# PEER dots that read the tile's activations from PSUM instead of SBUF, in a one-core DeepNorm encoder layer

## The chip, the cores and the metric

The kernel runs on one core of a Trainium2 chip. The metric is the device time of one execution in microseconds (us), smaller is better. Several executions are timed, and their median is the figure that is compared.

## What is computed

One post-norm encoder layer over 1024 positions of width 1024 in float32. The mixer half is multi-head attention (8 heads) beside a Fourier branch, merged by gates and projected. The second half is a retrieval layer (PEER), and it is where most bytes move: each position picks 128 of 16384 experts (8 heads, the best 16 each), and with its input `xc` (called h1 here), its experts `ec` and gates `gc`

```
u = jnp.take(w_u, ec, axis=0)
h = jnp.einsum('cd,ced->ce', xc, u, preferred_element_type=jnp.float32)
a = (jax.nn.gelu(h, approximate=False) * gc).astype(x.dtype)
return jnp.einsum('ce,ced->cd', a, jnp.take(w_v, ec, axis=0))
```

So every position needs 128 rows of `w_u` and 128 rows of `w_v`, each 4 KB, at data-dependent places.

## The kernel before, in words

The 1024 positions are four groups of 256; a group is two tiles of 128 positions (one position per partition). A prologue (input norm, latents, keys and values, Fourier branch) is followed by a long software pipeline. It is written out by hand as steps m = 0 to 255 per group: in step m of group g, every engine first does its part of one retrieval slot of group g and then its part of the front work (attention to routing) of group g+1. The instruction order of each engine is the order of these steps; the engines are held together by semaphores alone. A group before the first, called -1, runs only the front of group 0 beside the last part of the Fourier transform. The last group runs with no front beside it.

**The retrieval slots.** Slot i of a group is one expert per partition; slots 0 to 127 belong to tile 0, slots 128 to 255 to tile 1. For a slot, GpSimd (POOL) issues an indirect DMA for 128 rows of `w_u` (`gather_u`, L310, 76 slots ahead of m) and another for 128 rows of `w_v` (`gather_v`, L319, 64 ahead), both into rings of six buffers. Issuing one reads the column of row numbers `ids_peer` and makes the descriptors. VectorE (DVE) multiplies the landed u row by h1 and sums (`dot`, L872, in step m for slot m+76); its end frees the buffer for the gather six slots on. After eight dots ScalarE (ACT) does a Gelu, DVE multiplies by the gate (`coefs`, L883). ACT scales the v row into `av` (`scale`, L1099, two buffers), which frees the v buffer, and TensorE (PE) adds `av` to the accumulator in PSUM by eight transposing matmuls (L600).

**The front.** Attention goes head by head (u = 0 to 15: two tiles, eight heads), one head every four steps, in steps 0 to 70. Head u's steps, with a = 4u, are:

| step | engine and line | work |
|---|---|---|
| a (first tile only) | PE L467, DVE L752 to L755, ACT L1025 | queries of the head and their rotary part |
| a+2 | PE L483, DVE L760 | scores into `fA` (two banks), their maximum |
| a+3 | ACT L1030 | exponential of `fA` into `probs` |
| a+5 | PE L491 (recorded at its helper, L341), DVE L768 | `probs` turned into `fB` (two banks), copied to `probsT` |
| a+7 | PE L499 | probabilities times values |

So the next head's scores (step a+6) come one step after this head's turn. Steps 72 to 119 are gates and branch projections (L523, L535), 120 to 134 the output projection (L546), 136 to 146 the norm that gives h1, 148 to 212 the retrieval queries (L567) and key scores (L575). Weights come in 512 KB chunks through a ring of four. `retrieve` (DVE only, with `topk`, L734 to L742, and L813 to L861) finds the experts: tile 0 in steps 157 to 219, tile 1 in steps 27 to 117 of the following round, so beside the next group's attention. When the first quarter of a tile's lists is ready it copies h1 into `h1_peer` in SBUF (L855).

**PSUM** has eight banks, all of them in use: `acc` two (the retrieval accumulator), `fA` two, `fB` two, `m0` and `m1` one each. `m0` has the queries and the turned attention output, `m1` the attention output; both are free between step 72 and step 148.

Of the kernel before, what the change touches and what calls it, by code (L numbers as in the profile page):

```python
# [20 lines left out]
D = 1024  # L21
S = 1024
H, NOPE, ROPE, VD = 8, 64, 32, 64
# [7 lines left out]
KD = D // P  # L31
# [36 lines left out]
def layer_program(nc, x, lnp, w_lat, w_z, w_kr, b_lat, b_zT, b_krT, gqkv, w_uk, w_uv, b_gate, wstream,  # L68
# [4 lines left out]
    with ctx:  # L73
# [99 lines left out]
            return ctx.enter_context(nc.psum_tensor(name, [P, n], fp32))  # L173

        acc = ps("acc", D)
        fA, fB = ps("fA", 1024), ps("fB", 1024)
        m0, m1 = ps("m0", 512), ps("m1", 512)
        banks = (fA[:, 0:512], fA[:, 512:1024], fB[:, 0:512], fB[:, 512:1024])

        cos_part, sin_part = acc[:, 0:512], acc[:, 512:1024]  # L180

# [155 lines left out]
        def _(pe):  # L337
# [108 lines left out]
            def front(g, m):  # L446

                for u in range(TILES * H):
                    a = A0 + A_PERIOD * u
                    qt, h = divmod(u, H)  # L450
                    if m == a and qt == 0:
                        c0 = WQ0 + 2 * (h // 4)
                        if h == 0:
                            pe.wait_ge(q_in, 32 * g + 32)
                        if h % 4 == 0:
                            chunk(g, c0)
                            chunk(g, c0 + 1)
                        if positive(g * H + h):
                            pe.wait_ge(q_nope, g * H + h)
                        if positive(g * H + h):  # L460
                            pe.wait_ge(q_rope, g * H + h)
                        if h == 0:
                            if positive(g * 2 * PH):
                                pe.wait_ge(s_sb, g * 2 * PH)
                        o = (h % 4) * P
                        for k in range(2):
                            last = mm(m0[:, 0:GROUP], wring[:, (c0 + k) % NW, o:o + P], cqT_g[:, k, :],  # L467
                                      start=k == 0, stop=k == 1)
                        last.then_inc(q_ps, 1)
                        if h % 4 == 3:  # L470
                            pe.drain().then_inc(w_free, 1)
                            pe.drain().then_inc(w_free, 1)
                    if m == a + 2:
                        if qt == 0:
                            pe.wait_ge(q_nope, g * H + h + 1)
                            pe.wait_ge(q_rope, g * H + h + 1)
                        if positive(g * TILES * H + u):
                            pe.wait_ge(probs_sb, g * TILES * H + u)
                        if u == 0:
                            if positive(g * TILES):  # L480
                                pe.wait_ge(h1T_sb, g * TILES)
                        for half in range(2):
                            last = mm(fA[:, half * 512:(half + 1) * 512], qT_g[0:QK, h, tok(qt)],  # L483
                                      KT[0:QK, h, half * 512:(half + 1) * 512], start=True, stop=True)
                        last.then_inc(scores_ps, 1)
                    if m == a + 5:
                        pe.wait_ge(probs_sb, g * TILES * H + u + 1)
                        if positive(g * TILES * H + u):
                            pe.wait_ge(probsT_sb, g * TILES * H + u)
                        for k in range(TT):  # L490
                            last = tr(fB[:, tok(k)], probs[:, tok(k)])  # L491
                        last.then_inc(probsT_ps, 1)
                    if m == a + 7:
                        pe.wait_ge(probsT_sb, g * TILES * H + u + 1)
                        if h == 0:
                            if positive(g * TILES + qt):
                                pe.wait_ge(o_done, g * TILES + qt)
                        for k in range(TT):
                            last = mm(m1[:, h * VD:(h + 1) * VD], probsT[:, tok(k)], V[:, k, h * VD:(h + 1) * VD],  # L499
                                      start=k == 0, stop=k == TT - 1)  # L500
                        last.then_inc(pv_ps, 1)
                    if h == H - 1 and m == a + 9:
                        pe.wait_ge(o_done, g * TILES + qt + 1)
                        if positive(g * TILES + qt):
                            pe.wait_ge(oT_sb, g * TILES + qt)
                        for c in range(4):
                            last = tr(m0[:, tok(c)], o_sb[:, tok(c)])
                        last.then_inc(oT_ps, 1)

                for dc in range(KD):  # L510
                    a = M0 + M_PERIOD * dc
                    gb, yb = banks[dc % 2], banks[2 + dc % 2]
                    for j in range(2):
                        if m == a + 2 * j:
                            if dc == 0 and j == 0:
# [23 lines left out]
                for k in range(KD):  # L539
                    if m == O0 + 2 * k:  # L540
                        if k == 0:
                            pe.wait_ge(m_done, (g + 1) * KD)
                        w = chunk(g, WO0 + k)
                        for t in range(TILES):
                            for half in range(2):
                                last = mm(banks[2 * t + half], mT[:, k, tok(t)], w[:, half * 512:(half + 1) * 512],  # L546
                                          start=k == 0, stop=k == KD - 1)
                        last.then_inc(w_free, 1)

                for t in range(TILES):  # L550
                    if m == L0 + 4 + 4 * t:
                        pe.wait_ge(h1_done, g * TILES + t + 1)
                        for k in range(KD):
                            last = tr((fA, fB)[t][:, tok(k)], h1_front[:, t, tok(k)])
                        last.then_inc(h1T_ps, 1)

                for qc in range(2 * PH):
# [73 lines left out]
        def _(dve):  # L631
# [112 lines left out]
            def front(g, m):  # L744
                for u in range(TILES * H):
# [18 lines left out]
                    if m == a + 5:  # L764
                        dve.wait_ge(probsT_ps, g * TILES * H + u + 1)
                        if positive(g * TILES * H + u):
                            dve.wait_ge(pv_ps, g * TILES * H + u)
                        v.tensor_copy(probsT, fB[:, :]).then_inc(probsT_sb, 1)  # L768
                    if h == H - 1 and m == a + 8:
                        dve.wait_ge(pv_ps, g * TILES * H + u + 1)  # L770
                        if positive(g * TILES + qt):
# [7 lines left out]
                for dc in range(KD):  # L779
                    if m == M0 + M_PERIOD * dc + 5:  # L780
                        dve.wait_ge(gates_sb, g * KD + dc + 1)
                        dve.wait_ge(w_free, used(g, WM0 + 3 * dc + 2))
                        v.tensor_tensor(prod[:, :, :].rearrange("p a b -> p (a b)"),  # L783
                                        sg[:, :, :].rearrange("p a b -> p (a b)"), banks[2 + dc % 2], ALU.mult)
                        dve.drain()
                        v.tensor_tensor(mT[:, dc, :], prod[:, 0, :], prod[:, 1, :], ALU.add).then_inc(m_done, 1)
                        dve.drain()
                for t in range(TILES):
                    if m == L0 + 4 * t:
                        if t == 0:  # L790
                            dve.wait_ge(w_free, used(g, WP0 - 1))
                            dve.wait_ge(hres_in, 16 * (g + 1))
                        v.tensor_tensor(h1_front[:, t, :], h1_front[:, t, :], (fA, fB)[t][:, :], ALU.add)
                        dve.drain()
                        stats(1, h1_front[:, t, :], var1)
                    if m == L0 + 4 * t + 2:
# [69 lines left out]
            def dot(g, i):  # L866
                g, i = slot_of(g, i)
                t = i // SLOTS
                dve.wait_ge(u_in[ring(g, i, NU)], landed(g, i, NU))
                row = u_rows[:, ring(g, i, NU), :]  # L870
                b = i // BATCH % 2
                v.tensor_tensor_reduce(out=row, in0=row, in1=h1_peer[:, t, :], scale=1.0, scalar=0.0, op0=ALU.mult,  # L872
                                       op1=ALU.add, accum_out=dots[:, b, i % BATCH:i % BATCH + 1]).then_inc(u_free, 1)

            def coefs(g, k):
# [68 lines left out]
        def _(act):  # L944
# [71 lines left out]
            def front(g, m):  # L1016
# [24 lines left out]
                for dc in range(KD):  # L1041
                    if m == M0 + M_PERIOD * dc + 3:
# [1 line left out]
                        if positive(g * KD + dc):  # L1044
                            act.wait_ge(m_done, g * KD + dc)
                        for j in range(2):
                            last = s.activation(sg[:, j, :], banks[dc % 2][:, j * GROUP:(j + 1) * GROUP], ACT.Sigmoid,
                                                bias=bg[:, j, dc:dc + 1])
                        last.then_inc(gates_sb, 1)
                if m == HAND1 + 2:  # L1050
# [4 lines left out]
                for t in range(TILES):  # L1055
# [2 lines left out]
                        s.activation(sd[:, 1, 1:2], sd[:, 1, 0:1], ACT.Sqrt).then_inc(std1, 1)  # L1058
                    if m == L0 + 4 * t + 6:
                        act.wait_ge(h1T_ps, g * TILES + t + 1)  # L1060
                        s.activation(hT_g[:, :, tok(t)], (fA, fB)[t][:, :].rearrange("p (k t) -> p k t", k=KD),  # L1061
                                     ACT.Copy).then_inc(h1T_sb, 1)
                for qc in range(2 * PH):
                    a = K0 + K_PERIOD * qc
# [182 lines left out]
```

## Time and profile before

| | |
|---|---|
| median of 3 runs | 3676.09 us (3662.14 to 3679.78) |
| profiled execution, its own time | 3666.81 us |
| its span, first to last instruction | 3665.0 us |
| PE matmul busy | 2779.8 us, 76% |
| POOL busy | 2356.0 us, 64% |
| DVE busy | 2220.9 us, 61% |
| ACT busy | 1612.2 us, 44% |
| bytes moved by DMA | 1240.83 MB, of them 1073.87 MB by POOL's gathers |

Busy time counts an instruction from its start to its end; waiting for a semaphore is not in it. The profile cuts the span into 40 slices: the DMA engines are busy from slice 7 on (about 550 us), when the first gathers go out, until the end, and move between 317 and 409 GB/s there. The first 550 us are the prologue and the front of group 0.

### The profile page before, as it was taken

What the parts mean: (1) busy time and instruction counts of PE and PEld (TensorE: products, weight loads), DVE (VectorE), ACT (ScalarE), POOL (GpSimd) and SP (SyncE); (2) the same over time, 40 slices, a digit from 0 to 9 for tenths busy, and PEclk for the clock granted to TensorE, in tenths of its full rate; (3) what the DMA queues carried; (4) which work ended last, traced back from release to release, by engine and by line L of the source; (5) the groups of instructions that cost most, each with busy time, mean ns of one, the idle gap of its engine ahead of it and who ended that gap; (6) DMA issues with size and microseconds to landing.
All of it is one profiled execution on the core that took longest, in us unless ns stands there. A gap on an engine that the chain in (4) does not pass through costs nothing.

```text
span 3665.0 us, 40824 instructions
## 1 busy us (share of the span) xinstructions
PE 2779.8 (76%) x14008; PEld 2205.7 (60%) x14008; DVE 2220.9 (61%) x5004; ACT 1612.2 (44%) x1842; POOL 2356.0 (64%) x2075
## 2 busy tenths in 40 slices
PE   6999986667788776677788776678787776666676
PEld 3456855556676565556675665567775665555555
DVE  5044148547865578457765686477765785466643
ACT  1121013445554555455554554455454454444444
POOL 3000007766677777766778787666777777777775
PEclk9999997578799898587899896687899985655556
DMA  4224539999999999999999999999999999999998
GB/s 170 92 92 144 172 125 341 384 344 327 330 399 409 409 409 386 376 340 317 360 409 409 409 393 376 374 338 328 373 409 409 409 382 373 408 364 357 359 396 344
DMA packets 350432, 1240.83 MB, mean 339 GB/s; under 512 B 38480, under 2 KB 46160, under 8 KB 349712
## 3 DMA queue, kind: packets, MB, share of 16 engines
q0 software_dynamic: 294912, 1073.87, 76.7%
q1 hardware_dynamic: 34096, 117.94, 8.8%
q10 hardware_dynamic: 21216, 46.40, 3.6%
q8 instruction: 111, 1.82, 0.2%
q14 instruction: 97, 0.79, 0.1%
HBM read 1222.33 MB, written 15.73 MB: 338 GB/s over the span
## 4 chain that ended last, share of the span: by engine, by line
POOL 29%; PE 24%; DMA 18%; issue 11%; DVE 8%; ACT 5%; DVEq 3%; SPq 0%; ACTq 0%; POOLq 0%
DMA rows<-in_peer_v,ids_peer 17%; POOL rows L310 15%; POOL rows L319 15%; PE acc L600 5%; ACT av L1099 4%; PE fA L483 3%; PE m L567 2%; PE fA L523 2%; PE m L371 2%; DVE small L760 2%; PE acc L589 1%; PE fB L341 1%; DVE rows L872 1%; PE m L467 1%; PE m L499 1%
## 5 line engine op out<-in xcount | busy, mean ns | idle before, releaser
L600 PE MATMUL acc<-ident,av 128*128 128x128 f32 x8192 | 1471.9, 340 | 762.1 <-ACT av L1099 747.5
L600 PEld LDWEIGHTS acc<-ident,av 128*128 128x128 f32 x8192 | 1212.0, 176 | 1036.0 <-ACT av L1099 965.1
L310 POOL DMA_INDIRECT rows<-in_peer_u,ids_peer x1024 | 1151.3, 1124 | 828.2 <-DVE ids_peer L852 348.9
L872 DVE CUSTOM_DVE_ANT_0 rows<-rows,hh 128x1024 f32<-128x1024 f32 x1024 | 1241.9, 1222 | 698.1 <-DMA rows<-in_peer_u,ids_peer 687.2
L1099 ACT ACTIVATE av<-rows,coef 128x1024 f32<-128x1024 f32 x1024 | 1164.2, 1145 | 1107.8 <-DMA rows<-in_peer_v,ids_peer 1001.6
L319 POOL DMA_INDIRECT rows<-in_peer_v,ids_peer x1024 | 1156.7, 1130 | 318.9 <-issue 278.1
L567 PE MATMUL m<-hT_g,wring 128*128 128x256 f32 x1024 | 254.3, 406 | 1.1 <-ACT hT_g L1061 1.1
L523 PE MATMUL fA<-hT_g,wring 128*128 128x256 f32 x1024 | 233.7, 383 | 0.0
L567 PEld LDWEIGHTS m<-hT_g,wring 128*128 128x128 f32 x1024 | 206.9, 208 | 31.2 <-ACT hT_g L1061 1.5
L523 PEld LDWEIGHTS fA<-hT_g,wring 128*128 128x128 f32 x1024 | 193.3, 193 | 24.9
L1030 ACT ACTIVATE S<-fA,small 128x1024 f32<-128x1024 f32 x64 | 71.3, 1114 | 266.1 <-DVE small L762 266.1
L499 PEld LDWEIGHTS m<-V,S 128*128 128x128 f32 x1024 | 128.9, 203 | 18.1 <-DVE S L768 10.9
L768 DVE COPY S<-fB 128x1024 f32<-128x1024 f32 x64 | 78.2, 1222 | 100.2 <-PE fB L341 98.6
L499 PE MATMUL m<-V,S 128*128 128x64 f32 x1024 | 130.4, 284 | 9.3 <-DVE S L768 9.3
L483 PE MATMUL fA<-KT,hT_g 96*128 96x512 f32 x256 | 122.8, 602 | 0.0
L535 PE MATMUL fB<-yo,wring 128*128 128x256 f32 x512 | 115.8, 379 | 0.0
L760 DVE TENSOR_REDUCE small<-fA 128x1 f32<-128x1024 f32 x64 | 78.3, 1223 | 53.0 <-PE fA L483 52.9
L535 PEld LDWEIGHTS fB<-yo,wring 128*128 128x128 f32 x512 | 95.4, 190 | 12.0
L1090 ACT ACT_TABLE_LOAD x76 | 97.5, 1283 | 1.4
L783 DVE TENSOR_TENSOR prod<-sg,fB 128x512 f32<-128x512 f32 x32 | 21.8, 682 | 121.5 <-PE fB L535 121.5
L1069 ACT ACTIVATE qcT<-m 128x256 f32<-128x256 f32 x64 | 24.5, 383 | 152.6 <-PE m L567 152.6
L341 PE MATMUL fB<-ident,S 128*128 128x128 f32 x512 | 88.1, 330 | 1.0 <-issue 0.8
(153 smaller groups left out, 2183.2 us busy)
## 6 DMA issues: line engine op xcount, KB each, us to landing
wring<-in_wstream SPq DMA_DIRECT2D x192, 512.0 KB
ln<-in_dft_seq ACTq DMA_DIRECT2D x32, 512.0 KB, 3.5
rows<-in_peer_u,ids_peer POOLq DMA_INDIRECT x1024, 7.1
rows<-in_peer_v,ids_peer POOLq DMA_INDIRECT x1024, 7.1
hT_g<-in_x SPq DMA_DIRECT2D x8, 512.0 KB, 3.6
hres_spill<-KT ACTq DMA_DIRECT2D x8, 512.0 KB, 2.7
hT_spill<-rows ACTq DMA_DIRECT2D x1, 4096.0 KB, 11.1
wring<-in_wstream SPq DMA_DIRECT2D x16, 256.0 KB
```

The source lines that it names most:

```text
L310: pool.indirect_dma_start(u_rows[:, ring(g, i, NU), :], None, peer_u, bass.IndirectOffsetOnAxis(ap=ids_peer[:, t, s:s + 1], axis=0)).then_ ...
L319: pool.indirect_dma_start(v_rows[:, ring(g, i, NV), :], None, peer_v, bass.IndirectOffsetOnAxis(ap=ids_peer[:, t, s:s + 1], axis=0)).then_ ...
L341: return nc.tensor.transpose(out_, in_, ident[:, :])
L483: last = mm(fA[:, half * 512:(half + 1) * 512], qT_g[0:QK, h, tok(qt)], KT[0:QK, h, half * 512:(half + 1) * 512], start=True, stop=True)
L499: last = mm(m1[:, h * VD:(h + 1) * VD], probsT[:, tok(k)], V[:, k, h * VD:(h + 1) * VD], start=k == 0, stop=k == TT - 1)
L523: last = mm(gb[:, j * GROUP:(j + 1) * GROUP], w[:, tok(k)], hT_g[:, k, :], start=k == 0, stop=k == KD - 1)
L535: last = mm(yb[:, j * GROUP:(j + 1) * GROUP], w[:, tok(4 * j + k)], src[:, k, :], start=k == 0, stop=k == 3)
L567: last = mm(m0[:, (qc % 2) * GROUP:(qc % 2 + 1) * GROUP], w[:, tok(k)], hT_g[:, k, :], start=k == 0, stop=k == KD - 1)
L600: last = mm(acc[:, tok(k)], av[:, i % NAV, tok(k)], ident[:, :], is_transpose=True, start=i % SLOTS == 0 and k % 4 == 0, stop=i % SLOTS == ...
L760: v.reduce_max(nmax[:, u % 2:u % 2 + 1], fA[:, :], AX)
L872: v.tensor_tensor_reduce(out=row, in0=row, in1=h1_peer[:, t, :], scale=1.0, scalar=0.0, op0=ALU.mult, op1=ALU.add, accum_out=dots[:, b, i ...
L1099: s.activation(av[:, i % NAV, :], v_rows[:, ring(g, i, NV), :], ACT.Copy, scale=coef[:, b, i % BATCH:i % BATCH + 1]).then_inc(scaled, 1)
```

## The change

The two banks of `fB` become `h1_ps`. Before the first dot of each tile DVE copies that tile's h1 from SBUF to `h1_ps`, and all 128 dots of the tile take it from there; the u row, in and out, stays in SBUF. What used `fB` has to move: the gates' partner banks, the output projection of tile 1 and its turned h1 go to `m0` and `m1`, which become one tensor `mB`. The turned probabilities go to `fA`, the banks of the scores, in the fronts of groups 1 to 3 (in the front of group 0, which ends its attention before the first dot, they stay where they were). For that PE gets a new wait: before the scores of head u it waits until head u-1's turned probabilities have been copied out of `fA` (`probsT_sb`).

```
-        fA, fB = ps("fA", 1024), ps("fB", 1024)
-        m0, m1 = ps("m0", 512), ps("m1", 512)
-        banks = (fA[:, 0:512], fA[:, 512:1024], fB[:, 0:512], fB[:, 512:1024])
+        fA, h1_ps, mB = ps("fA", 1024), ps("h1_ps", D), ps("mB", 1024)
+        m0, m1 = mB[:, 0:512], mB[:, 512:1024]
+        banks = (fA[:, 0:512], fA[:, 512:1024], h1_ps[:, 0:512], h1_ps[:, 512:1024])
+        fbanks = (fA[:, 0:512], fA[:, 512:1024], m0, m1)
+        def turned(g):
+            return h1_ps if isinstance(g, int) and g == 0 else fA
...
+                        if u > 0 and turned(g) is fA:
+                            pe.wait_ge(probsT_sb, g * TILES * H + u)
                         for half in range(2):
                             last = mm(fA[:, half * 512:(half + 1) * 512], qT_g[0:QK, h, tok(qt)],
...
-                            last = tr(fB[:, tok(k)], probs[:, tok(k)])
+                            last = tr(turned(g)[:, tok(k)], probs[:, tok(k)])
...
-                    gb, yb = banks[dc % 2], banks[2 + dc % 2]
+                    gb, yb = fbanks[dc % 2], fbanks[2 + dc % 2]
...
-                                last = mm(banks[2 * t + half], mT[:, k, tok(t)], w[:, half * 512:(half + 1) * 512],
+                                last = mm(fbanks[2 * t + half], mT[:, k, tok(t)], w[:, half * 512:(half + 1) * 512],
...
-                            last = tr((fA, fB)[t][:, tok(k)], h1_front[:, t, tok(k)])
+                            last = tr((fA, mB)[t][:, tok(k)], h1_front[:, t, tok(k)])
...
-                        v.tensor_copy(probsT, fB[:, :]).then_inc(probsT_sb, 1)
+                        v.tensor_copy(probsT, turned(g)[:, :]).then_inc(probsT_sb, 1)
...
                 dve.wait_ge(u_in[ring(g, i, NU)], landed(g, i, NU))
+                if i % SLOTS == 0:
+                    dve.drain()
+                    v.tensor_copy(h1_ps[:, :], h1_peer[:, t, :])
+                    dve.drain()
...
-                v.tensor_tensor_reduce(out=row, in0=row, in1=h1_peer[:, t, :], scale=1.0, scalar=0.0, op0=ALU.mult,
+                v.tensor_tensor_reduce(out=row, in0=row, in1=h1_ps[:, :], scale=1.0, scalar=0.0, op0=ALU.mult,
```

The gate and norm lines of DVE and ACT change their bank in the same way.

## Rows read from the trace of the kernel before

**Rows 1.** The page, costliest groups: line, engine, operation | busy us, mean ns | idle before
```profile
L310 POOL DMA_INDIRECT rows<-in_peer_u,ids_peer x1024 | 1151.3, 1124 | 828.2 <-DVE ids_peer L852 348.9
L872 DVE CUSTOM_DVE_ANT_0 rows<-rows,hh 128x1024 f32<-128x1024 f32 x1024 | 1241.9, 1222 | 698.1 <-DMA rows<-in_peer_u,ids_peer 687.2
...
L319 POOL DMA_INDIRECT rows<-in_peer_v,ids_peer x1024 | 1156.7, 1130 | 318.9 <-issue 278.1
...
L768 DVE COPY S<-fB 128x1024 f32<-128x1024 f32 x64 | 78.2, 1222 | 100.2 <-PE fB L341 98.6
```
**Rows 2.** Stretches: length; busy us (x) of PE, PEld, DVE, ACT, POOL; PEclk; DMA share, GB/s
```profile
548.00:650.00 102.00, 67.73 (x340) 56.96 (x339) 83.45 (x237) 38.20 (x50) 72.84 (x61) 0.77 0.94 349
650.00:757.00 107.00, 66.75 (x313) 53.77 (x313) 55.19 (x104) 48.03 (x47) 82.61 (x81) 0.63 1.00 388
...
1552.00:1802.00 250.00, 186.59 (x1086) 157.72 (x1086) 177.40 (x371) 131.34 (x149) 165.22 (x148) 0.80 0.94 334
1802.00:2037.00 235.00, 192.23 (x1064) 155.45 (x1063) 147.78 (x330) 119.57 (x125) 184.94 (x153) 0.96 1.02 405
2037.00:2164.00 127.00, 95.85 (x571) 82.85 (x570) 91.26 (x246) 63.83 (x78) 99.82 (x85) 0.93 1.02 401
2164.00:2256.00 92.00, 63.52 (x360) 53.84 (x359) 73.94 (x192) 48.21 (x56) 73.11 (x62) 0.82 0.99 379
2256.00:2344.00 88.00, 61.55 (x266) 49.32 (x266) 41.34 (x71) 38.26 (x37) 67.55 (x68) 0.56 1.02 400
...
757.00:1552.00 795.00, 608.28 (x3338) 507.08 (x3338) 531.13 (x1207) 401.12 (x444) 570.88 (x511) 0.83 0.98 376
1552.00:2344.00 792.00, 599.73 (x3338) 499.18 (x3338) 531.71 (x1207) 401.21 (x444) 590.64 (x514) 0.85 0.99 378
2344.00:3137.00 793.00, 604.33 (x3336) 504.45 (x3334) 531.32 (x1206) 400.44 (x444) 592.57 (x512) 0.84 0.98 376
...
3220.00:3480.00 260.00, 168.00 (x719) 134.94 (x717) 176.78 (x440) 115.16 (x114) 202.51 (x177) 0.54 0.97 358
3480.00:3554.00 74.00, 52.13 (x216) 41.64 (x216) 33.77 (x59) 32.24 (x31) 56.83 (x56) 0.52 1.00 392
3554.00:3634.00 80.00, 59.13 (x249) 47.28 (x250) 38.56 (x67) 36.16 (x36) 60.99 (x63) 0.54 1.03 409
```
**Rows 3.** The chain of waits, share by line, 3220 to 3480 us (last group)
```profile
by line: POOL rows L319 31.2%; POOL rows L310 26.9%; issue 17.2%; DMA rows<-in_peer_v,ids_peer 12.9%; ACT av L1099 2.2%; PE acc L600 0.8%; PE acc L607 0.8%; DVEq L850 0.6%; DVE onehot L840 0.5%; DVE ybuf L648 0.5%; DVE ybuf L888 0.5%; DVE y
```
**Rows 4.** The chain of waits, share by line, 1667 to 1776 us (attention of group 2)
```profile
by line: PE acc L600 17.9%; issue 10.3%; DVE rows L872 8.4%; PE fA L483 8.0%; DVE small L760 7.7%; PE fB L341 7.0%; ACT av L1099 4.8%; ACT L1090 2.3%; DVE S L768 2.2%; DVEq L811 2.1%; DVEq L735 2.1%; DVEq L737 2.0%; DVEq L739 1.9%; DVE si L
```
**Rows 5.** POOL's two lines over the whole run: ns min/median/max
```profile
L310 POOL DMA_INDIRECT rows<-in_peer_u,ids_peer x1024: 933/940/2130, 540.2 to 3627.4; - x171
...
L319 POOL DMA_INDIRECT rows<-in_peer_v,ids_peer x1024: 932/939/2202, 568.5 to 3645.4; - x171
```
**Rows 6.** Timeline at 1722.8 us: start us, us, engine, line (a gather issued beside a dot)
```profile
1722.86 1.22 DVE L872 CUSTOM_DVE_ANT_0 rows<-rows,hh 128x1024 f32<-128x1024 f32 x1
1722.90 1.98 POOL L310 DMA_INDIRECT rows<-in_peer_u,ids_peer  x1 [0.30 <-issue]
```
**Rows 7.** Timeline at 1226.4 us (a gather issued beside an SBUF plus PSUM sum)
```profile
1226.48 1.21 DVE L793 TENSOR_TENSOR hh<-hh,fB 128x1024 f32<-128x1024 f32 x1
1226.54 0.94 POOL L310 DMA_INDIRECT rows<-in_peer_u,ids_peer  x1 [0.30 <-issue]
```
**Rows 8.** Timeline at 2387 us, one head of attention: PE and DVE
```profile
2386.81 1.04 PE L341 MATMUL fB<-ident,S 128*128 128x128 f32 x8
...
2387.69 1.04 PE L600 MATMUL acc<-ident,av 128*128 128x128 f32 x8
2387.89 1.23 DVE L768 COPY S<-fB 128x1024 f32<-128x1024 f32 x1 [0.75 <-PE fB L341]
2388.45 0.30 PEld L483 LDWEIGHTS fA<-KT,hT_g 96*128 96x128 f32 x2
2388.56 1.88 PE L483 MATMUL fA<-KT,hT_g 96*128 96x512 f32 x4
...
2390.48 1.22 DVE L760 TENSOR_REDUCE small<-fA 128x1 f32<-128x1024 f32 x1 [0.23 <-PE fA L483]
```
**Rows 9.** Timeline at 2450 us, a head whose copy comes late behind retrieval
```profile
2450.58 0.30 PEld L483 LDWEIGHTS fA<-KT,hT_g 96*128 96x128 f32 x2
...
2454.38 1.22 DVE L768 COPY S<-fB 128x1024 f32<-128x1024 f32 x1
2455.66 2.65 PEld L499 LDWEIGHTS m<-V,S 128*128 128x128 f32 x13 [2.45 <-DVE S L768]
...
2456.66 1.22 DVE L760 TENSOR_REDUCE small<-fA 128x1 f32<-128x1024 f32 x1
```
**Rows 10.** DVE groups by shape: busy us, mean ns | idle before
```profile
L644 DVE SCALAR_TENSOR_TENSOR hh<-hh,small,ln 128x1024 f32<-128x1024 f32 x8 | 10.2, 1280 | 0.0
L888 DVE SCALAR_TENSOR_TENSOR ybuf<-hh,acc 128x1024 f32<-128x1024 f32 x8 | 9.7, 1218 | 20.9 <-PE acc L607 20.9
L855 DVE COPY hh<-hh 128x1024 f32<-128x1024 f32 x8 | 5.6, 696 | 0.0
```
**Rows 11.** Waits, 3220 to 3480 us: total us, times, longest
```profile
DVE rows L872 <- DMA rows<-in_peer_u,ids_peer: 67.8, 45, 2.5
```

More of the change, by code:

```diff
@@ L783, in front @@
                         v.tensor_tensor(prod[:, :, :].rearrange("p a b -> p (a b)"),
-                                        sg[:, :, :].rearrange("p a b -> p (a b)"), banks[2 + dc % 2], ALU.mult)
+                                        sg[:, :, :].rearrange("p a b -> p (a b)"), fbanks[2 + dc % 2], ALU.mult)
                         dve.drain()
@@ L792, in front @@
                             dve.wait_ge(hres_in, 16 * (g + 1))
-                        v.tensor_tensor(h1_front[:, t, :], h1_front[:, t, :], (fA, fB)[t][:, :], ALU.add)
+                        v.tensor_tensor(h1_front[:, t, :], h1_front[:, t, :], (fA, mB)[t][:, :], ALU.add)
                         dve.drain()
@@ L1046, in front @@
                         for j in range(2):
-                            last = s.activation(sg[:, j, :], banks[dc % 2][:, j * GROUP:(j + 1) * GROUP], ACT.Sigmoid,
+                            last = s.activation(sg[:, j, :], fbanks[dc % 2][:, j * GROUP:(j + 1) * GROUP], ACT.Sigmoid,
                                                 bias=bg[:, j, dc:dc + 1])
@@ L1060, in front @@
                         act.wait_ge(h1T_ps, g * TILES + t + 1)
-                        s.activation(hT_g[:, :, tok(t)], (fA, fB)[t][:, :].rearrange("p (k t) -> p k t", k=KD),
+                        s.activation(hT_g[:, :, tok(t)], (fA, mB)[t][:, :].rearrange("p (k t) -> p k t", k=KD),
                                      ACT.Copy).then_inc(h1T_sb, 1)
```

## The prediction

> **What bounds the kernel now.** I read the costliest groups first. POOL issues 1024 gathers for u and 1024 for v, at means of 1124 and 1130 ns; a dot on DVE takes 1222 ns [rows 1]. But half of all issues take 940 ns or less, and the longest over 2100 [rows 5]. The mean is pulled up by a part of the issues that are nearly a dot longer. The timeline shows which: an issue that starts 0.04 us after a dot takes 1.98 us [rows 6]. It ends 0.80 us after that dot does, as if it had got almost nothing done beside it. Next to a sum of the same size that has one input in SBUF and the other in PSUM, the issue takes 0.94 us [rows 7]. So what POOL waits for is DVE's second SBUF input. Over the run this is 1024 x (1124 - 940) + 1024 x (1130 - 939) ns = 384 us of POOL time.
>
> POOL is busy in 64% of the span, so next I asked where it is on the path. The table by stretches gives DMA's rate [rows 2]; 409 GB/s is the highest anywhere, and the reader should see that it is reached in quite different stages, so I take it as the ceiling. One steady group is 1552 to 2344 us; the two others (757 to 1552, 2344 to 3137) have its length within 3 us and its rate within 2 GB/s. Its attention (1552 to 1802) runs at 334 GB/s, the gates and projections at 405, the routing stretches at 401, 379 and 400. In the last group, with retrieval of tile 1 alone beside the slots (3220 to 3480), the rate is 358. There the chain of waits is POOL: 58% in its two lines and 17% in the issue time between them [rows 3]. In attention it is another chain: PE, DVE and ACT in turn, no POOL line among its leading entries [rows 4]. That is the ring scores, maximum, exponential, scaling, accumulating, turning, scores; a gather that comes earlier doesn't shorten it.
>
> **The change part by part.**
>
> *The dots free POOL (gain).* If issues fall to 940 ns beside every dot, POOL could do a slot in 2 x (0.94 + 0.30) = 2.48 us, the 0.30 being the issue gap [rows 6]. A slot's two gathers are 1.049 MB, 2.56 us at 409 GB/s, so DMA becomes the bound wherever POOL was. The most a stretch can give is its length x (1 - rate/409), for the same bytes. After attention in a steady group: 235 us at 405 gives 2.3, 127 at 401 gives 2.5, 92 at 379 gives 6.7, 88 at 400 gives 1.9; 13.4 together, 40 for three groups. Last group: 260 at 358 gives 32.4, 74 at 392 gives 3.1; 36. First slots: 107 at 388 gives 5.5, and 102 at 349 gives 15, of which I take a third, for DVE is 82% busy there [rows 2]. Upper end 96 us. A check from the other side: in 3220 to 3480 POOL's 177 issues took 202.5 us and would take 166, 36 us less, of which the ceiling lets 32 through. I take 85% of 40 and 36, since DVE's retrieval bursts leave gaps: 34 + 31 + 5 + 5 = 75 us. Lower end: half, 38.
>
> *Attention gets a link (loss).* Before, scores of head u+1 went into `fA` while head u's turned probabilities lay in `fB`. Now they wait for DVE's copy. In an ordinary head [rows 8] the turn ends at 2387.85; PE does a slot's accumulation meanwhile and loads weights for the scores at 2388.45. The copy ends at 2389.12, and PE starts about 0.05 after a copy's end, from 2455.60 to 2455.66 in [rows 9]. So the scores start at 2389.17, 0.72 later. DVE had nothing to do but wait for them, so the maximum comes 0.72 later, and with it the whole ring. Queued behind the waiting scores on PE are the next slot's accumulation and the value product, which waited for the same copy anyway. Where retrieval makes the copy late [rows 9], the scores wait 5.1 us (2450.58 to 2455.66), but DVE reaches the maximum late too: new scores end at 2457.5 against a maximum that began at 2456.66, 0.9 late. Other heads lie between 0.1 and 1.0; I take 0.65. Per group 15 heads have a predecessor, in three groups 45: 29 us. The front of group 0 keeps its old banks and costs nothing. Lower end: a third of it (10), should other slack in the ring take it up. Upper end: some four heads a group pass on 3 us each: 3 x (11 x 0.65 + 4 x 3) = 57.
>
> *The copies.* Eight, SBUF to PSUM, 128x1024. The trace has none; PSUM to SBUF takes 1222 ns [rows 1], SBUF to SBUF 696 [rows 10]. PSUM on one side makes the first the nearer; with two drains 1.4 us. The four for tile 0 (step 180) and the last for tile 1 lie where DVE waits for u rows (67.8 us in 260 in the last group [rows 11]) and cost nothing; without that cover each is 1.4 us. The three for tile 1 at step 52 fall into attention: about 1 us each, 3 us (0 to 4).
>
> *The dots themselves.* With a PSUM input a comparable two-input operation takes 1218 ns, with SBUF alone 1280 [rows 10]. The dot is at 1222 already; I leave it, between -60 and +60 ns. In attention 8.4% of the chain is dots [rows 4], so 5% on them is 3 us either way over 750 us; elsewhere they are covered. (The Trainium skill, VectorE: DVE Perf Modes, section on the TRN2 errata, gives VectorE a larger fixed cost from PSUM than from SBUF, 120 against 58 cycles at 0.96 GHz. By that estimate a dot is 65 ns longer and the sum 3 us worse; the rows on the sum with a PSUM input show no such excess.)
>
> *Moved banks.* Gates, output projection and the turned h1 use `m0` and `m1` when attention is over; their existing waits already cover it. Same instructions, same order: 0.
>
> **Sum.** -75 + 29 + 3 = -43 us on the profiled execution's own 3666.8 us: 3624. The median shown is 9 us higher; within that spread I give 3625.
>
> **The rivals.**
>
> *The late copies pass on in full.* Speaks for it: in attention everything hangs together, and retrieval is also on the chain. Against: the maximum was late as well [rows 9]. 3667 - 75 + 57 + 3 = 3652, no change.
>
> *The freed time stays off the path.* Only the lower gain comes, because gathers already fill DMA whenever they can. For it: DMA is called 97% busy even at 358 GB/s [rows 2]. Against: the chain there is POOL's. 3667 - 38 + 29 + 3 = 3661, no change.
>
> *Slower: the hold isn't lifted.* POOL would be held by the dot as such (its own kind of operation, u row in and out in SBUF), not by its second SBUF input. Then nothing is gained, and attention's link remains: 3667 + 32 = 3699. Rows 7 speak against it, but with a plain sum, not a dot. It decides if issues beside dots stay above 1100 ns in the mean. This is also how the change could fail to do what it says. (The Trainium skill, SBUF — State Buffer, section on who interferes with whom, says that a two-input VectorE operation holds up only GpSimd's reads, and infers that making descriptors needs only the write side and so isn't stalled by it. By that the change gains nothing, 3699 too. The 1.98 us issue beside a dot contradicts it, unless the reading of row numbers is what is held.)
>
> *Better: the link is hidden* in attention, or costs 10: 3667 - 90 + 10 = 3587.
>
> **How the numbers follow.** Forecast 0.60; late copies in full 0.13; gain off the path 0.10; hold not lifted 0.10; hidden link 0.07. Within 0.5% (18 us, about what this measurement tells from no change) lie the two middle rivals, less a part of each: 0.19. Slower: the third rival and the bad end of the second, 0.13. Faster: 0.68. Range: upper end of the gain with a small loss, 3590; above it takes in the late copies and the unhelped path, 3668. Left out are the hold not lifted and half of the best case.
>
> **What would show it.** Right: both POOL lines at about 940 to 960 ns in the mean; 3220 to 3480 shortened by some 28 us, at 400 GB/s or more; the attention stretch of each steady group longer by 9 to 12 us, with PE waiting for the copy in front of L483's line. Wrong: issue times as before; attention longer by 19 us or more; the rate still under 380 with fast issues, which would mean a loop between DVE and the six buffers bounds instead. Dots above 1290 ns would put retrieval on the path.

## The result and the profile after

The changed kernel takes 3636.6 us in the median (3625.2 to 3637.2, four runs) against 3677.9 for the kernel before in the same comparison (3662.1 to 3681.0); the ratio is 0.9885, 95% interval 0.9852 to 0.9917. That is 41 us less, and the interval of the ratio allows 31 to 54; 43 were forecast. The time itself was forecast at 3625 and is 12 us above it, nearly all because the prediction started from a profiled execution of 3666.8 us, which is 11 below the kernel's median here. The two profiled executions have spans of 3665.0 and 3634.6 us, only 30 apart, since the one of after lies at its kernel's median. Sums over stretches below are of those two.

The gather lines and the dot on the page after (line engine op, shapes and count | busy us, mean ns | idle before). They answer to [rows 1]; the code has moved, so L310 is L316, L319 is L325, L872 is L884:

```profile
L884 DVE CUSTOM_DVE_ANT_0 rows<-rows,h_ps 128x1024 f32<-128x1024 f32 x1024 | 1234.4, 1216 | 620.0 <-DMA rows<-in_peer_u,ids_peer 608.2
L316 POOL DMA_INDIRECT rows<-in_peer_u,ids_peer x1024 | 984.7, 962 | 1103.8 <-DVE dots L884 568.0
L325 POOL DMA_INDIRECT rows<-in_peer_v,ids_peer x1024 | 964.9, 942 | 371.1 <-issue 244.3
```

An issue takes 962 and 942 ns in the mean where it took 1124 and 1130. POOL got back 358 of the 384 us that the prediction counted, and what it got back became waiting for dots: 568 us, where it had been 203. The gathers go out earlier and stay under way longer, 11.9 us from issue to landing in the median for `w_u` rows, where it was 7.1. The dot is 6 ns shorter with its PSUM input.

The stretches of after (length; busy us of PE, PEld, DVE, ACT, POOL with counts; PEclk; DMA share, GB/s), cut at the same dots as those of before:

```profile
550.00:745.00 195.00, 126.58 (x646) 105.04 (x645) 137.39 (x339) 85.81 (x96) 136.57 (x144) 0.74 1.00 391
...
1542.00:1807.00 265.00, 191.62 (x1078) 155.01 (x1079) 178.88 (x372) 130.11 (x148) 136.09 (x143) 0.81 0.87 309
1807.00:2041.00 234.00, 191.50 (x1069) 154.91 (x1067) 146.46 (x329) 119.85 (x126) 145.42 (x153) 0.97 1.02 407
2041.00:2341.00 300.00, 216.85 (x1192) 182.78 (x1192) 206.79 (x508) 150.33 (x172) 206.70 (x218) 0.82 1.03 408
...
3216.00:3452.00 236.00, 154.76 (x715) 125.17 (x716) 176.74 (x443) 115.03 (x115) 168.06 (x177) 0.63 1.00 394
3452.00:3603.00 151.00, 112.28 (x471) 89.66 (x469) 72.62 (x125) 68.10 (x66) 107.72 (x115) 0.53 1.03 409
```

Against [rows 2], by the times of the same dots: the first slots gave 14 us (209 to 195, with 391 GB/s in place of 369), the stretches after attention 9, 8 and 12 us in the three groups, 28 before rounding (routing now at 406 to 409 GB/s), the last group 27 (of it 23 or 24 between 3216 and 3452). That is 69 us gained. The three attention stretches went the other way, from 253, 250 and 251 us to 265, 265 and 262: 36 lost by the dots' times, 38 by these whole numbers. The chain of waits of 3216 to 3452, which answers to [rows 3]:

```profile
by line: DMA rows<-in_peer_u,ids_peer 19.4%; POOL rows L316 11.9%; POOL rows L325 11.6%; issue 11.5%; DVE rows L884 8.9%; DMA rows<-in_peer_v,ids_peer 8.0%; DVEq L858 2.0%; DVEq L819 2.0%; DVEq L745 1.9%; DVEq L747 1.8%; DVE onehot L848 1.8
```

POOL's two lines fell from 58% to 24% of it; transfers and dots took over, and the rate of 394 is 15 under the highest.

One head of attention after, near the place of [rows 8] (timeline):

```profile
2398.08 1.04 PE L608 MATMUL acc<-ident,av 128*128 128x128 f32 x8
2398.28 1.23 DVE L776 COPY S<-fA 128x1024 f32<-128x1024 f32 x1 [0.68 <-PE fA L347]
...
2399.63 0.30 PEld L491 LDWEIGHTS fA<-KT,hT_g 96*128 96x128 f32 x2 [0.74 <-issue]
2399.66 1.95 PE L491 MATMUL fA<-KT,hT_g 96*128 96x512 f32 x4 [0.54 <-DVE S L776]
...
2401.65 1.22 DVE L768 TENSOR_REDUCE small<-fA 128x1 f32<-128x1024 f32 x1 [1.00 <-PE fA L491]
```

The copy ends at 2399.51 and the scores' weights are loaded at 2399.63. From the copy's start to that load it was 0.56 us in [rows 8]; here it is 1.35, so 0.79 more. DVE then waits 1.00 us for the scores, where it had waited 0.23.

A head whose copy comes late looks different. This is the head of [rows 9] in the changed kernel (timeline):

```profile
2456.74 1.20 DVE L776 COPY S<-fA 128x1024 f32<-128x1024 f32 x1
...
2458.09 3.75 PE L491 MATMUL fA<-KT,hT_g 96*128 96x512 f32 x4 [5.07 <-DVE S L776]
...
2461.88 1.23 DVE L768 TENSOR_REDUCE small<-fA 128x1 f32<-128x1024 f32 x1 [2.80 <-PE fA L491]
```

PE has waited 5.07 us for the copy, and then the scores take 3.75 us, where they took 1.88 before. The stretch of just these scores shows the TensorE clock that was granted, 0.50 of full speed, which is the 1.2 GHz level. The first line is of the changed kernel, the second of the same head's scores in the kernel before, at 1.00 (2.4 GHz):

```profile
2458.09:2461.84 3.75, 3.75 (x5) 1.58 (x6) 0.99 (x2) 0.00 (x0) 1.87 (x2) 0.50 0.71 234
```
```profile
2450.69:2452.57 1.88, 1.88 (x8) 0.87 (x7) 1.57 (x7) 0.97 (x1) 1.14 (x1) 1.00 0.95 373
```

So the next maximum begins 3.94 us after this copy's end; in [rows 9] it was 1.06. Taking the same times for all 45 heads that have a predecessor in their group (groups 1 to 3):

| mean, end of the copy to start of the next maximum | before | after |
|---|---|---|
| 33 heads, copy right behind the turn | 1.46 us | 2.17 us |
| 12 heads, four a group, copy late behind retrieval | 1.29 us | 3.87 us |

The 33 cost 0.71 each, the 12 cost 2.58 each: 23 + 31 = 54 us more at this link. Only 36 to 38 of it reached the length of attention; where the rest was made up isn't shown. In all of the 12, and in no head of the kernel before, the scores take over 3 us: PE has waited 3.0 to 5.4 us for the copy, and the clock is at 0.50 when they start (9 heads) or falls to it during them (3). The mean granted clock of the stretch did not fall (0.82, 0.81 and 0.84, before 0.77, 0.80 and 0.78); but slow moments now lie on the ring. In the chain of waits of 1660 to 1790 us the scores' line has 18.9%, where [rows 4] shows 8.0%.

### The profile page after: what moved, and what is told of

Same layout as the page of the kernel before. It is cut to its first block, busy times and chain, and to the rows that moved or that the text cites. A ratio compares the mean times of both kernels' runs of the same rounds, so it can differ in the third digit from the quotient of the medians.

```text
span 3634.6 us, 40893 instructions
## 1 busy us (share of the span) xinstructions
PE 2734.6 (75%) x14008; PEld 2148.4 (59%) x14008; DVE 2223.7 (61%) x5012; ACT 1610.4 (44%) x1842; POOL 1997.5 (55%) x2075
## 4 chain that ended last, share of the span: by engine, by line
PE 27%; DMA 26%; DVE 14%; POOL 12%; issue 9%; DVEq 6%; ACT 5%; SPq 0%; ACTq 0%; POOLq 0%
DMA rows<-in_peer_v,ids_peer 19%; POOL rows L316 6%; POOL rows L325 6%; DMA rows<-in_peer_u,ids_peer 6%; PE acc L608 5%; ACT av L1111 4%; PE fA L491 4%; PE fA L531 3%; DVE rows L884 3%; PE mB L575 2%; PE mB L543 2%; PE mB L377 2%; PE acc L597 2%; DVE small L768 1%; DVE S L776 1%
## 5 line engine op out<-in xcount | busy, mean ns | idle before, releaser
L608 PE MATMUL acc<-ident,av 128*128 128x128 f32 x8192 | 1408.9, 329 | 713.0 <-ACT av L1111 697.4
L884 DVE CUSTOM_DVE_ANT_0 rows<-rows,h_ps 128x1024 f32<-128x1024 f32 x1024 | 1234.4, 1216 | 620.0 <-DMA rows<-in_peer_u,ids_peer 608.2
L316 POOL DMA_INDIRECT rows<-in_peer_u,ids_peer x1024 | 984.7, 962 | 1103.8 <-DVE dots L884 568.0
L325 POOL DMA_INDIRECT rows<-in_peer_v,ids_peer x1024 | 964.9, 942 | 371.1 <-issue 244.3
L575 PE MATMUL mB<-hT_g,wring 128*128 128x256 f32 x1024 | 259.1, 411 | 1.1 <-ACT hT_g L1073 1.1
L575 PEld LDWEIGHTS mB<-hT_g,wring 128*128 128x128 f32 x1024 | 210.2, 211 | 32.8 <-ACT hT_g L1073 1.5
L507 PEld LDWEIGHTS mB<-V,S 128*128 128x128 f32 x1024 | 132.0, 207 | 10.1 <-issue 7.2
L507 PE MATMUL mB<-V,S 128*128 128x64 f32 x1024 | 132.0, 286 | 2.7 <-DVE S L776 2.7
L543 PE MATMUL mB<-yo,wring 128*128 128x256 f32 x512 | 115.8, 379 | 0.0
L543 PEld LDWEIGHTS mB<-yo,wring 128*128 128x128 f32 x512 | 95.4, 190 | 12.0
## 6 DMA issues: line engine op xcount, KB each, us to landing
rows<-in_peer_u,ids_peer POOLq DMA_INDIRECT x1024, 11.9
```

Of the source, the lines that this page charges most:

```text
L316: pool.indirect_dma_start(u_rows[:, ring(g, i, NU), :], None, peer_u, bass.IndirectOffsetOnAxis(ap=ids_peer[:, t, s:s + 1], axis=0)).then_ ...
L325: pool.indirect_dma_start(v_rows[:, ring(g, i, NV), :], None, peer_v, bass.IndirectOffsetOnAxis(ap=ids_peer[:, t, s:s + 1], axis=0)).then_ ...
L543: last = mm(yb[:, j * GROUP:(j + 1) * GROUP], w[:, tok(4 * j + k)], src[:, k, :], start=k == 0, stop=k == 3)
L575: last = mm(m0[:, (qc % 2) * GROUP:(qc % 2 + 1) * GROUP], w[:, tok(k)], hT_g[:, k, :], start=k == 0, stop=k == KD - 1)
L608: last = mm(acc[:, tok(k)], av[:, i % NAV, tok(k)], ident[:, :], is_transpose=True, start=i % SLOTS == 0 and k % 4 == 0, stop=i % SLOTS == ...
L884: v.tensor_tensor_reduce(out=row, in0=row, in1=h1_ps[:, :], scale=1.0, scalar=0.0, op0=ALU.mult, op1=ALU.add, accum_out=dots[:, b, i % BAT ...
```

## The experiments

**Dots from SBUF again (e1_sbuf_dots).** Banks, wait and copies stay as changed.

```
-  v.tensor_tensor_reduce(out=row, in0=row, in1=h1_ps[:, :], ...
+  v.tensor_tensor_reduce(out=row, in0=row, in1=h1_peer[:, t, :], ...
```

> The changed kernel with its banks, its new wait and its eight copies, but the dots read h1 from SBUF again. Theory (the dots' second SBUF input holds POOL's issues, and that is the whole gain; the wait in attention is the whole loss): both gather lines back at 1120 to 1135 ns in the mean, attention of each steady group still 261 to 265 us, the routing stretches and the last group as in the kernel before, the time about 3678 + 36 + 2 = 3716 us, ratio 1.008 to 1.012. Rival (the gain is from the moved banks, not from the operand): gather lines may be slow again but the time stays near 3637, ratio 0.99.

Measured: 3705.3 us against 3676.1 for the kernel before, ratio 1.0082 (1.0057 to 1.0107). The issues are slow again, 1110 and 1141 ns. Attention is nearly as long as in the changed kernel (784 us in the three stretches, there 792), and the last group is as in the kernel before; POOL's two lines are 64% of its chain again:

```profile
751.00:1014.00 263.00, 184.58 (x1077) 148.66 (x1078) 179.47 (x372) 130.01 (x148) 159.16 (x146) 0.84 0.88 316
1550.00:1812.00 262.00, 187.26 (x1073) 152.23 (x1073) 178.86 (x372) 129.60 (x148) 157.98 (x146) 0.82 0.89 317
2362.00:2621.00 259.00, 185.44 (x1073) 150.20 (x1072) 178.69 (x372) 129.64 (x148) 159.39 (x148) 0.83 0.89 321
3250.00:3509.00 259.00, 166.13 (x718) 133.48 (x719) 178.07 (x443) 115.28 (x115) 202.71 (x177) 0.55 0.97 359
```

It splits the change into its two parts: everything but the operand costs 29 us (the interval allows 21 to 39), and the operand alone gives 3705.3 - 3636.6 = 69. The two kernels were timed in different comparisons; by their ratios to the kernel before it is 72, give or take 15. The rival that the moved banks bring the gain is out. The loss is 9 us less than the 38 expected, inside the interval.

**The copy in two halves (e2_split_copy).** In the changed kernel, PE signals after four and after eight turns, DVE copies 512 columns at a time, and each half of the scores waits for its own half.

```
                         for k in range(TT):
                             last = tr(turned(g)[:, tok(k)], probs[:, tok(k)])
+                            if k % 4 == 3:
+                                last.then_inc(probsT_ps, 1)
...
-                            pe.wait_ge(probsT_sb, g * TILES * H + u)
+                            pe.wait_ge(probsT_sb, 2 * (g * TILES * H + u) - 1)
                         for half in range(2):
+                            if half == 1 and u > 0 and turned(g) is fA:
+                                pe.wait_ge(probsT_sb, 2 * (g * TILES * H + u))
...
-                        v.tensor_copy(probsT, turned(g)[:, :]).then_inc(probsT_sb, 1)
+                        for half in range(2):
+                            cols = slice(half * 512, (half + 1) * 512)
+                            dve.wait_ge(probsT_ps, 2 * (g * TILES * H + u) + half + 1)
...
+                            v.tensor_copy(probsT[:, cols], turned(g)[:, cols]).then_inc(probsT_sb, 1)
```

The other waits on these two semaphores count in twos as well.

> The changed kernel with each turned head copied out in two halves, signalled apart: the first half of the scores waits only for the first half's copy, and that copy starts after four of the eight turns. Theory (the scores' wait for the copy is what attention loses): the first half is free about 0.7 us earlier than the whole was, so most of the 0.7 to 0.8 us a head goes; attention 252 to 256 us a group instead of 261 to 265, the time 3637 - 25 = about 3612 us, ratio 0.980 to 0.985. Rival (attention lost its time through retrieval's late copies, or through gathers competing): attention stays at 260 or more and the extra 0.16 us of DVE a head makes the time 3637 to 3645, ratio 0.989 to 0.991.

Measured: 3597.8 us, ratio to the kernel before 0.9785 (0.9759 to 0.9811), whose interval lies wholly below that of the changed kernel. It beats both kernels: 78 us under the one before, 39 under the changed one. The attention stretches:

```profile
750.00:1002.00 252.00, 186.28 (x1080) 154.27 (x1078) 180.45 (x390) 130.61 (x148) 136.62 (x142) 0.81 0.90 329
1535.00:1790.00 255.00, 188.53 (x1074) 155.17 (x1074) 179.95 (x388) 129.73 (x148) 135.97 (x142) 0.80 0.89 320
2325.00:2576.00 251.00, 179.72 (x1079) 147.31 (x1078) 179.74 (x388) 130.26 (x148) 136.16 (x142) 0.84 0.90 324
```

They are 758 us together, where the changed kernel has 792 and the kernel before 754. One head there (timeline):

```profile
793.76 1.51 PE L347 MATMUL fA<-ident,S 128*128 128x128 f32 x8
794.86 1.29 DVE L781 COPY S<-fA 128x512 f32<-128x512 f32 x2 [1.61 <-PE fA L347]
795.88 0.30 PEld L493 LDWEIGHTS fA<-KT,hT_g 96*128 96x128 f32 x2
```

DVE starts copying at 794.86, before the eight turns are through at 795.27, and PE loads the scores' weights at 795.88, before both halves are out at 796.15. The scores are no longer behind the whole copy, and in the 33 ordinary heads PE no longer waits before them at all. In the 12 late ones it still waits, 2.8 to 5.3 us. The time gained is more than the 25 us expected. The profiled pair is 29 us apart, with 34 gained in attention; the difference to 39 is within what executions differ by. Heads whose scores take over 3 us are 7 here and 12 in the changed kernel, a part of the gain that the expectation didn't have; its size isn't separated.

**The copy a step later (e3_later_copy).** DVE copies the turned head at step a+6, behind the next dot.

```
-                    if m == a + 5:
+                    if m == a + 6:
                         dve.wait_ge(probsT_ps, g * TILES * H + u + 1)
```

> The changed kernel with DVE's copy of a turned head moved one step on, behind the next slot's dot. It doubles the suspected wait: the scores are later by a dot, 1.2 us, in each of 45 heads. Theory: attention longer by 45 x 1.2 / 3 = 18 us a group (279 to 283), the time 3637 + 54 = about 3690 us, ratio 1.000 to 1.006. Rival (the ring has slack and attention's loss is something else): under 5 us a group, the time under 3655, ratio under 0.995.

Measured: 3654.2 us, ratio 0.9932 (0.9907 to 0.9957), so 17.5 us above the changed kernel and neither theory's number. The three attention stretches are 270, 268 and 269 us, 15 more than in the changed kernel. Idle time of DVE ahead of the copy (us, times), changed kernel first, then this one:

```profile
  PE fA L347: 60.1, 33
...
  PE fA L491: 65.9, 43
```
```profile
  PE fA L347: 25.7, 17
...
  PE fA L491: 84.2, 44
```

The second line of each is PE waiting for the copy before the scores. In the changed kernel DVE often stood waiting for PE's turns; with the copy moved the dot sits in that gap and fills 34 us of it. 45 heads times 1.22 us is 55, less 34 is 21, near the 15 to 17.5 measured; PE's wait grew by 18. So the ring passes the delay on, but my count overlooked that a wait can be filled; delay counts only beyond the slack of the link it is put into.

**The product to PSUM (e4_product_to_psum).** Both inputs in SBUF, as before the change, only the write leaves SBUF. It has a drain before each dot and no copies of h1.

```
-                if i % SLOTS == 0:
-                    dve.drain()
-                    v.tensor_copy(h1_ps[:, :], h1_peer[:, t, :])
-                    dve.drain()
...
-                v.tensor_tensor_reduce(out=row, in0=row, in1=h1_ps[:, :], ...
+                dve.drain()
+                v.tensor_tensor_reduce(out=h1_ps[:, :], in0=row, in1=h1_peer[:, t, :], ...
```

> The dots take both inputs from SBUF and write the product to PSUM (with a drain in front of each dot, since all write the same place, and without the eight copies of h1). It tells the read side from the write side. Theory (the second SBUF input is what holds POOL): gather lines 1120 to 1140 ns in the mean, an issue beside a dot near 1.9 us, the time 3715 to 3740 us. Rival (the write of the product to SBUF, or its combination with two reads, holds POOL): gather lines 940 to 970 ns, the time 3640 to 3660 us.

Measured: 3696.2 us, ratio 1.0054 (1.0030 to 1.0078), and issues of 1116 and 1100 ns. The page's lines, then two moments of its timeline:

```profile
L316 POOL DMA_INDIRECT rows<-in_peer_u,ids_peer x1024 | 1143.1, 1116 | 891.2 <-DVE ids_peer L860 348.2
L881 DVE CUSTOM_DVE_ANT_0 h_ps<-rows,hh 128x1024 f32<-128x1024 f32 x1024 | 1264.3, 1235 | 662.7 <-DMA rows<-in_peer_u,ids_peer 577.0
L325 POOL DMA_INDIRECT rows<-in_peer_v,ids_peer x1024 | 1126.3, 1100 | 314.4 <-issue 235.2
```
```profile
769.41 1.23 DVE L881 CUSTOM_DVE_ANT_0 h_ps<-rows,hh 128x1024 f32<-128x1024 f32 x1
769.55 1.90 POOL L316 DMA_INDIRECT rows<-in_peer_u,ids_peer  x1 [4.94 <-DVE dots L881]
...
800.58 1.26 DVE L881 CUSTOM_DVE_ANT_0 h_ps<-rows,hh 128x1024 f32<-128x1024 f32 x1
800.58 0.94 POOL L325 DMA_INDIRECT rows<-in_peer_v,ids_peer  x1 [0.30 <-issue]
```

A dot that writes nothing big to SBUF holds an issue just as long: 1.90 us beside it. The changed kernel's dot has one read and the write in SBUF and doesn't hold it, so it is the two reads. The time is 19 us or more below what was expected, and 9 below e1_sbuf_dots; this kernel has no copies of h1 and its issues are a little shorter, and I did not take that difference apart.

**Splitting alone (e5_split_alone).** The kernel before, with only the halved copy and its signals, as in e2_split_copy (turned heads stay in `fB`, the scores don't wait).

```
+                            if k % 4 == 3:
+                                last.then_inc(probsT_ps, 1)
...
+                            v.tensor_copy(probsT[:, cols], fB[:, cols]).then_inc(probsT_sb, 1)
```

> The kernel before (h1 in SBUF, turned heads in fB, no wait of the scores for the copy) with the copy in two halves. It asks whether e2's gain over the changed kernel is the wait taken away, or a shorter way to the value product that any kernel would have. Theory (the copy was on no ring before): attention 250 to 254 us a group as before, plus up to 1 us for the extra 0.16 us a head; the time 3676 to 3682 us, ratio 1.000 to 1.002. Rival (the value product's early start pays by itself): attention 240 to 247, the time under 3660, ratio under 0.996.

Measured: 3678.3 us, ratio 1.0013 (0.9990 to 1.0036), no change. Attention was 246, 249 and 251 us in the profiled run; the 8 us less there than before don't show in the time. So what the split gains in the changed kernel comes from the wait, not from splitting as such. No head's scores take over 3 us here, as in the kernel before: without the wait for the copy they don't occur.

**Five copies (e6_five_copies).**

```
-                    v.tensor_copy(h1_ps[:, :], h1_peer[:, t, :])
-                    dve.drain()
+                    for _ in range(5):
+                        v.tensor_copy(h1_ps[:, :], h1_peer[:, t, :])
+                        dve.drain()
```

> The changed kernel with each tile's copy of h1 to PSUM made five times in place of once: 32 more copies, each with its drain about 1.3 us, 5.2 us more in one place per tile. Theory (copies outside attention are covered by DVE's waits for rows, the three in attention cost about 1 us each): the three in attention 3 x 5 = 15 us at most, the others nothing or 1 us each; the time 3640 to 3657 us. Rival (a stop of DVE always reaches the end, since six buffers are soon empty): 8 x 5.2 = 42 us, the time 3675 to 3680.

Measured: 3656.7 us, ratio 0.9951 (0.9929 to 0.9973), 20 us more than the changed kernel (24 by the ratios, give or take 14): at the upper end of the theory and half of the rival's 42. In the profiled run 9 us of the growth lie in attention (801 against 792), and one copy takes 1228 ns. A fourth of 20 us is 5 for the eight real copies; the prediction had 3, and the two aren't told apart.

**PSUM only beside attention (e8_psum_in_attention).**

```
+                in_attention = g < GROUPS - 1 and 76 <= i < 76 + 72
+                h1 = h1_ps[:, :] if in_attention else h1_peer[:, t, :]
-                v.tensor_tensor_reduce(out=row, in0=row, in1=h1_ps[:, :], ...
+                v.tensor_tensor_reduce(out=row, in0=row, in1=h1, ...
```

> The changed kernel, but only the dots of steps 0 to 71 beside a next group's attention (216 of 1024) read h1 from PSUM; all others read it from SBUF as in e1_sbuf_dots. It asks where free issues pay. Theory (attention is bound by the ring over PE, DVE and ACT, not by POOL): POOL's issues are fast there and slow elsewhere, attention 260 to 265 us a group, the time that of e1_sbuf_dots, 3700 to 3712, ratio 1.006 to 1.010. Rival (attention is helped as well, and the changed kernel's loss there is a larger wait less a gain): 216/1024 of the 68 us or more come back, the time 3691 or less, ratio under 1.005.

Measured: 3698.4 us, ratio 1.0075 (1.0046 to 1.0103), where e1_sbuf_dots has 1.0082. One stretch of attention and one of the last group:

```profile
759.00:1022.00 263.00, 188.91 (x1086) 153.93 (x1087) 179.71 (x374) 131.20 (x150) 141.77 (x148) 0.82 0.89 318
...
3244.00:3501.00 257.00, 164.38 (x714) 131.96 (x713) 177.27 (x440) 115.17 (x114) 199.98 (x176) 0.57 0.97 361
```

Beside attention 148 POOL instructions took 142 us, 17 less than in e1_sbuf_dots, and the stretch is as long as there; the three together are 781 us, there 784. Free issues pay little or nothing where the ring bounds. The time is 2 us below what was expected, the ratio inside. The rival's ratio of under 1.005 just touches the interval, so the times alone make its 15 us unlikely and don't exclude them; the stretches show 3.

## Why the prediction was right

*The hold.* Forecast: issues at 940 to 960 ns. They are 962 and 942. That the second SBUF read is what holds them was argued from [rows 6] and [rows 7]; e1_sbuf_dots and e4_product_to_psum now show it. All issues of the traces agree: of those that start between 0.06 and 1.05 us behind a dot's start, the kernel before has 692, and they end 0.81 us (median; at least 0.80) after that dot's end, wherever in it they began; in the changed kernel 603 such issues take 0.93 to 0.95 us each. The Trainium skill (SBUF — State Buffer, section on who interferes with whom) has the first half of this right: a VectorE instruction with two SBUF inputs contends with a GpSimd one that reads SBUF. Its inference that descriptor generation isn't stalled by such an operation does not hold for these gathers, each of which also reads its row numbers; which part of the issue is held, no run here shows.

*The gain.* 75 forecast, 69 measured by e1_sbuf_dots against the changed kernel, and 69 by stretches. By place: last group 31 forecast, 27 found; after attention 34 and 28; first slots 10 and 14. The ceiling of 409 GB/s held in every stretch; routing and the last 150 us now run at it. One sign of being right was missed: the stretch of [rows 3] was to reach 400 GB/s or more and to be 28 us shorter; it reached 394 and is 23 or 24 shorter. DVE's dots (8.9%) and retrieval are in its chain now. The rival of a gain of only 38 is out.

*The loss.* 32 forecast (29 for the link, 3 for the copies). Measured 29 by e1_sbuf_dots, 36 to 38 by the attention stretches of the profiled pair, which grew by 12, 15 and 11 us (9 to 12 forecast). PE waits for the copy before 43 of the 45 scores. The ordinary heads are as worked out: 0.72 later by the prediction, 0.71 in the mean of 33. The late heads are not. The prediction let each pass on 0.1 to 1.0 us, since DVE is late there too, and they cost 2.58 at the link. The greater part is a term that it didn't have: it took the scores at their usual 1.88 us, and behind the long wait they ran at the 1.2 GHz level and took up to 3.75. The second thing it left out goes the other way: a third of the 54 us at the link did not reach the length of attention. That 32 came out is for this part luck. e2_split_copy suggests that it is the late heads' time that is made up, since they still wait there and its attention is within 4 us of the kernel before; no run separates the two. The rival of late copies had some four heads a group at 3 us and 57 us for the link, which is nearly what the link shows; but it passed all of it on, to 3652 us, and that e1_sbuf_dots excludes (60 with the copies, against 21 to 39).

*The sum.* 43 against 41 is closer than the numbers carry: the interval is 31 to 54, the gain came out 6 under and the loss, by e1_sbuf_dots, 3 under. The mechanism of the gain and its places are right; the loss is right in size and for ordinary heads.

*The others.* The hold was lifted, so the slower rival is out. The kernel with a hidden link (3587 forecast as the better case) is near what e2_split_copy is, 3598, but the change as made did not hide it.

## What to carry to other kernels

When DVE and POOL's gathers run side by side, give DVE's second operand a home in PSUM if it is used often: one copy for 128 dots pays at once. But look at where POOL is on the path: the stretches gained up to the DMA ceiling, and attention, whose chain is not POOL's, gained little or nothing. And when two buffers become one, pass it over in halves: nearly all of what looked like the price of the bank went away with two signals per head. Last, read the granted clock of what runs behind a new wait of PE: here the scores behind the long waits took twice as long.

## What the runs showed that was not expected

Who is first matters. In e4_product_to_psum an issue that starts in the same 0.01 us as a dot takes its plain 0.94 us, and the dot takes 1.26 instead of 1.23; an issue 0.14 us behind a dot takes 1.90. The kernel before shows the same: 19 issues that start 0 to 0.04 us behind a dot's start take 0.93 to 0.95 us, and it is the dot that is longer, 1.26 to 1.29 us. And a delay of 1.2 us per head, put on the ring, cost only a third of its sum (17.5 of 55 us), since the engine that got it had been idle for 60 us at that very link.
